# Attention heads: a third score buffer, one buffer for turned weights and value results, second scores in pieces

## The reference

```python
s = jnp.einsum('bqgrd,bkgd->bgrqk', qi, k).astype(jnp.float32) * scale
p = jax.nn.softmax(s, axis=-1).astype(v.dtype)
return jnp.einsum('bgrqk,bkgv->bqgrv', p, v)
```

## Time and profile before

| | us |
|---|---|
| median of 3 runs (2863.75 to 2866.16) | 2863.81 |
| the profiled execution | 2862.11 |
| its span, first to last instruction | 2860.3 |
| TensorE matmuls busy | 2600.9 (91%) |
| VectorE busy | 1240.2 (43%) |
| ScalarE busy | 1085.9 (38%) |
| GpSimd busy | 809.8 (28%) |
| DMA from HBM | 183.88 MB, mean 66 GB/s |

### The profile page before, as it was taken

How to read it: one execution, slowest core, us unless ns; L and a number is a source line. 1 busy time by engine, 2 the same in 40 slices (tenths; PEclk the granted TensorE clock), 3 DMA queues, 4 the chain that set the end, 5 groups by cost and what they waited for, 6 DMA issues and landing times. The chain is left out here.

```text
span 2860.3 us, 49221 instructions
## 1 busy us (share of the span) xinstructions
PE 2600.9 (91%) x19266; PEld 2041.7 (71%) x19266; DVE 1240.2 (43%) x1839; ACT 1085.9 (38%) x1682; POOL 809.8 (28%) x342
## 2 busy tenths in 40 slices
PE   8999979989898979888999999989978888998987
PEld 6887857868686857776778887767855566776665
DVE  3222024455655537344242220055846642584652
ACT  4443224343434323553233442233344422335441
POOL 3444433313232313112434444412210002232002
PEclk9999989999999989999999999999999999999998
DMA  4232322212121212111423233311110001121001
GB/s 135 90 95 92 105 66 86 91 52 83 59 83 59 83 39 74 52 38 59 134 82 95 88 95 98 100 37 53 55 41 1 1 9 51 52 74 59 1 1 66
DMA packets 52005, 188.49 MB, mean 66 GB/s; under 512 B 5760, under 2 KB 6016, under 8 KB 51712
## 3 DMA queue, kind: packets, MB, share of 16 engines
q1 hardware_dynamic: 50688, 181.74, 20.3%
q10 hardware_dynamic: 1152, 4.26, 0.4%
HBM read 183.88 MB, written 2.10 MB: 65 GB/s over the span
## 5 line engine op out<-in xcount | busy, mean ns | idle before, releaser
L2392 POOL TENSOR_TENSOR WLO<-RAW,WHI 128x1024 fp32r<-128x1024 f32 x334 | 804.7, 2409 | 2010.5 <-ACT WHI L299 2010.5
L299 ACT ACTIVATE WHI<-RAW 128x1024 fp32r<-128x1024 f32 x336 | 355.8, 1059 | 999.7 <-PE psum L313 708.8
L311 PE MATMUL psum<-HHI,WHI 128*128 128x512 f32 x872 | 353.8, 406 | 40.2 <-DVE HLO L397 15.0
L312 PE MATMUL psum<-HLO,WHI 128*128 128x512 f32 x872 | 347.0, 398 | 0.0
L313 PE MATMUL psum<-HHI,WLO 128*128 128x512 f32 x872 | 346.6, 397 | 0.0
L311 PE MATMUL psum<-H2HI,WHI 128*128 128x512 f32 (+1 forms) x536 | 197.3, 368 | 32.5 <-DVE H2LO L395 23.0
L311 PEld LDWEIGHTS psum<-HHI,WHI 128*128 128x128 f32 x872 | 165.8, 190 | 84.0 <-issue 43.9
L312 PEld LDWEIGHTS psum<-HLO,WHI 128*128 128x128 f32 x872 | 165.9, 190 | 41.7 <-issue 3.4
L313 PEld LDWEIGHTS psum<-HHI,WLO 128*128 128x128 f32 x872 | 165.7, 190 | 39.6
L312 PE MATMUL psum<-H2LO,WHI 128*128 128x512 f32 (+1 forms) x536 | 191.6, 357 | 0.0
L313 PE MATMUL psum<-H2HI,WLO 128*128 128x512 f32 (+1 forms) x536 | 191.2, 357 | 0.0
(11 more groups left out here) (394 smaller groups left out, 5196.6 us busy)
## 6 DMA issues: line engine op xcount, KB each, us to landing
RAW<-in_wstream SPq DMA_DIRECT2D x336, 512.0 KB, 3.5
X<-in_xT SPq DMA_DIRECT2D x8, 256.0 KB, 7.3
out_T<-OUT SPq DMA_DIRECT2D x4, 512.0 KB, 2.6
W3S<-in_lora ACTq DMA_DIRECT2D x5, 384.0 KB, 3.1
XC<-in_ctxT ACTq DMA_DIRECT2D x1, 1024.0 KB, 5.6
TRIG<-in_trig ACTq DMA_DIRECT2D x1, 960.0 KB, 7.6
FCC<-in_first SPq DMA_DIRECT2D x1, 576.0 KB, 9.0
LVL<-in_levels SPq DMA_DIRECT2D x1, 384.0 KB, 9.3
```

Of the source, the lines that this page charges most:

```text
L299: act.activation(WHI[:, q % 2, :], RAW[:, q % 2, :], ACT.Copy).then_inc(rounded, 1)
L311: pe.matmul(out, tile_of(WHI, slot, u), hi(kt), start=first and last[0], stop=False)
L312: pe.matmul(out, tile_of(WHI, slot, u), lo(kt), start=False, stop=False)
L2392: pool.tensor_tensor(WLO[:, s, :], RAW[:, s, :], WHI[:, s, :].bitcast(F32), ALU.subtract)\
```

## The change

There are three score buffers, `SCORES` = `two_banks` 0, 1 and 3, taken in turn by u % 3. There is one buffer for turned weights, `TURNED` = `two_banks[2]`, for even and odd units, and its columns 768 to 1023 hold the value results. So all turnings of an odd unit wait for the copy of the even one, and the turnings of an even unit for the copy of the odd unit before it. Its last two ("high") turnings, which share a bank with the value results, wait in addition for the result of the pair before.

TensorE's order for a pair with even unit u becomes: full scores of u + 2; values of the pair before; the four low turnings of u; the low scores (512 keys) of u + 3; the two high turnings of u; the high scores (256 keys) of u + 3; the six turnings of u + 1. The scores of units 0 and 1 stand ahead of the loop.

ScalarE does the exponents one unit ahead and then copies all 768 columns of a unit (256 for a context unit) in one instruction. VectorE copies no turned weights any more, and inverts the sums of a pair in one instruction of two columns. `heads_steps` is rewritten to these orders. The values wait for `ri` of the pair and for `pt` of the odd unit only.

```diff
@@ heads_tensor
+        SCORES, TURNED = (two_banks[0], two_banks[1], two_banks[3]), two_banks[2]
-            def scores(u):
+            def scores(u, ps):
...
-                    mm = pe.matmul(two_banks[a][:, at:at + w], lhs, rhs, start=True, stop=True)
-                mm.then_inc(*S.inc(f"sc{u}"))
+                    mm = pe.matmul(SCORES[u % 3][:, at:at + w], lhs, rhs, start=True, stop=True)
+                if ps and ps[-1][0]:
+                    mm.then_inc(*S.inc(f"sc{u}"))
             def values(j):
...
-                out = two_banks[3][:, TT:TT + 2 * P]
+                out = TURNED[:, TT:TT + 2 * P]
-                pe.wait_ge(*V.at(f"ri{2 * j + 1}"))
-                for u in (2 * j, 2 * j + 1):
-                    pe.wait_ge(*V.at(f"pt{u}"))
-                    pe.wait_ge(*A.at(f"pt{u}"))
+                pe.wait_ge(*V.at(f"ri{j}"))
+                pe.wait_ge(*A.at(f"pt{2 * j + 1}"))
...
-            scores(0)
-            for u, (kind, i, a, qb) in enumerate(us):
-                j = u // 2
-                if u + 1 < len(us):
-                    scores(u + 1)
-                if a == 0 and j:
-                    values(j - 1)
-                pe.wait_ge(*A.at(f"ex{u}"))
-                if a and j:
-                    pe.wait_ge(*V.at(f"y{j - 1}"))
-                pe.sem_inc(tensor_ready)
-                for b in keys_of(qb):
-                    mm = pe.transpose(two_banks[2 + a][:, b * P:(b + 1) * P], PX[:, a, b * P:(b + 1) * P], eye)
-                mm.then_inc(*S.inc(f"tr{u}"))
+            def turned(u, bs):
+                for b in bs:
+                    mm = pe.transpose(TURNED[:, b * P:(b + 1) * P], PX[:, us[u][2], b * P:(b + 1) * P], eye)
+                if KB - 1 in bs:
+                    mm.then_inc(*S.inc(f"tr{u}"))
+            LOW, HIGH = ((0, T),), ((T, TC),)
+            scores(0, LOW + HIGH)
+            scores(1, LOW + HIGH)
+            for u, (_, _, _, qb) in enumerate(us):
+                j, ahead = u // 2, u + 2 < len(us)
+                low, high = [b for b in keys_of(qb) if b < BLOCKS], [b for b in keys_of(qb) if b >= BLOCKS]
+                if u % 2 == 0:
+                    if ahead:
+                        if u:
+                            pe.wait_ge(*A.at(f"ex{u - 1}"))
+                        pe.sem_inc(tensor_ready)
+                        scores(u + 2, LOW + HIGH)
+                    if j:
+                        values(j - 1)
+                    pe.wait_ge(*A.at(f"ex{u}"))
+                    if u:
+                        pe.wait_ge(*A.at(f"pt{u - 1}"))
+                    pe.sem_inc(tensor_ready)
+                    if low:
+                        turned(u, low)
+                    if ahead:
+                        scores(u + 3, HIGH[:0] if us[u + 2][3] >= BLOCKS else LOW)
+                    if j:
+                        pe.wait_ge(*V.at(f"y{j - 1}"))
+                    pe.sem_inc(tensor_ready)
+                    turned(u, high)
+                    if ahead:
+                        scores(u + 3, HIGH)
+                else:
+                    pe.wait_ge(*A.at(f"ex{u}"))
+                    pe.wait_ge(*A.at(f"pt{u - 1}"))
+                    pe.sem_inc(tensor_ready)
+                    turned(u, low + high)
@@ heads_scalar
+            exponent(0)
             for u, (kind, i, a, qb) in enumerate(us):
...
+                if u + 1 < len(us):
+                    exponent(u + 1)
+                if a and j:
+                    rounded_part(j - 1)
                 act.wait_ge(*S.at(f"tr{u}"))
                 if j:
                     act.wait_ge(*S.at(f"pv{j - 1}"))
-                if qb < BLOCKS:
-                    act.activation(PTS[:, a, 0:T], two_banks[2 + a][:, 0:T], ACT.Copy).then_inc(*A.inc(f"pt{u}"))
-                else:
-                    act.sem_inc(A.inc(f"pt{u}")[0])
-                if a and j:
-                    rounded_part(j - 1)
+                act.activation(PTS[:, a, c0:], TURNED[:, c0:TT], ACT.Copy).then_inc(*A.inc(f"pt{u}"))
@@ heads_vector
             largest(0)
-            for u, (kind, i, a, qb) in enumerate(us):
+            largest(1)
+            for u in range(len(us)):
                 j = u // 2
-                if u:
-                    inverse(u - 1)
-                if u + 1 < len(us):
-                    largest(u + 1)
-                dve.wait_ge(*S.at(f"tr{u}"))
-                if j:
-                    dve.wait_ge(*S.at(f"pv{j - 1}"))
-                dve.tensor_copy(PTS[:, a, T:], two_banks[2 + a][:, T:TT]).then_inc(*V.inc(f"pt{u}"))
-                if j and not a:
+                if u % 2:
+                    inverse(j)
+                    if j:
+                        rest(j - 1)
+                if u + 2 < len(us):
+                    largest(u + 2)
+                if u % 2 == 0 and j:
                     result(j - 1)
-                if j and a:
-                    rest(j - 1)
```

More of the change, by code:

```diff
@@ L1696, in heads_steps @@
                 n = len(self.units())
-                pe, act, dve = ["sc0"], [], ["mx0", "nm0"]
+                pe, act, dve = ["sc0", "sc1"], ["ex0"], ["mx0", "nm0", "mx1", "nm1"]
                 for u in range(n):
-                    j = u // 2
-                    if u:
[L1701 to L1714, removed]
+                    j, ahead = u // 2, u + 2 < n
+                    if u % 2 == 0:
+                        pe += ([f"sc{u + 2}"] if ahead else []) + ([f"pv{j - 1}"] if j else []) + [f"tr{u}"]
+                        dve += ([f"mx{u + 2}", f"nm{u + 2}"] if ahead else []) + ([f"rg{j - 1}", f"y{j - 1}"] if j else [])
+                    else:
+                        pe += ([f"sc{u + 2}"] if ahead else []) + [f"tr{u}"]
+                        dve += [f"ri{j}"] + ([f"lo{j - 1}"] if j else []) + ([f"mx{u + 2}", f"nm{u + 2}"] if ahead else [])
+                    act += ([f"ex{u + 1}"] if u + 1 < n else []) + ([f"hi{j - 1}"] if u % 2 and j else []) + [f"pt{u}"]
                 j = n // 2 - 1
-                return pe + [f"pv{j}"], act + [f"hi{j}"], dve + [f"ri{n - 1}", f"rg{j}", f"y{j}", f"lo{j}"]
+                return pe + [f"pv{j}"], act + [f"hi{j}"], dve + [f"rg{j}", f"y{j}", f"lo{j}"]
         sa = Area(0)
@@ L2150, in heads_tensor @@
             st.enter(pe, "pe")
-            def scores(u):
+            def scores(u, ps):
                 kind, i, a, qb = us[u]
-                if u >= 2:
-                    pe.wait_ge(*A.at(f"ex{u - 2}"))
-                pe.sem_inc(tensor_ready)
                 hs = slice(a * HD, a * HD + HD)
                 qs = slice(qb * P, (qb + 1) * P)
-                for at, w in ((0, T), (T, TC)):
+                for at, w in ps:
                     if qb >= BLOCKS and not at:
@@ L2202, in heads_scalar, with exponent @@
             st.enter(act, "act")
+            def exponent(u):
+                kind, _, a, qb = us[u]
+                c0 = 0 if qb < BLOCKS else T
+                act.wait_ge(*V.at(f"nm{u}"))
+                if u >= 2:
+                    act.wait_ge(*S.at(f"tr{u - 2}"))
+                act.activation(PX[:, a, c0:], SCORES[u % 3][:, c0:TT], ACT.Exp, scale=scale_of(kind), bias=NM2[:, u % COLS:u % COLS + 1],
+                               accum_out=DEN2[:, u % COLS:u % COLS + 1]).then_inc(*A.inc(f"ex{u}"))
             def rounded_part(j):
@@ L2234, in largest, with inverse, part_of @@
                 dve.wait_ge(*S.at(f"sc{u}"))
-                dve.tensor_reduce(MX2[:, u % COLS:u % COLS + 1], two_banks[a][:, (0 if qb < BLOCKS else T):TT], AX, ALU.max).then_inc(*V.inc(f"mx{u}"))
+                dve.tensor_reduce(MX2[:, u % COLS:u % COLS + 1], SCORES[u % 3][:, (0 if qb < BLOCKS else T):TT], AX, ALU.max).then_inc(*V.inc(f"mx{u}"))
                 dve.wait_ge(*V.at(f"mx{u}"))
                 dve.tensor_scalar(NM2[:, u % COLS:u % COLS + 1], MX2[:, u % COLS:u % COLS + 1], -scale_of(kind), None, ALU.mult).then_inc(*V.inc(f"nm{u}"))
[L2238 to L2241, removed]
+            def inverse(j):
+                dve.wait_ge(*A.at(f"ex{2 * j + 1}"))
+                d = DEN2[:, 2 * j % COLS:2 * j % COLS + 2]
+                dve.reciprocal(d, d).then_inc(*V.inc(f"ri{j}"))
+            def part_of(t, j):
                 kind, i, _, qb = us[2 * j]
```

18 lines of the change are left out of this document (6 added, 12 removed).

## The result

The changed kernel takes **2863.75 us** (median of 20 runs, 2857.15 to 2870.12); the kernel before, run beside it, takes 2858.26 us (20 runs, 2852.22 to 2866.16). The ratio is 1.0019, 95% interval 1.0010 to 1.0027: 5.5 us slower, at the very edge (0.2%) of what I had said a measurement of this kernel can tell. The 2870.7 that I had forecast stands 12.4 us above the 2858.26 of before. The profiled execution of after took 2864.55 us, 2.4 more than that of before (2862.11).

The account below looks back on a forecast made before the run. TensorE, busy for 91% of the span, was taken as the bound. Layer 1's heads +4.9 us and layer 0's +2.0 made +6.9 on a profiled 2862.1, or 2869.0; 1.7 more for the median gave 2870.7 us, range 2860 to 2879.

Parts of the forecast that it names:

- the median of the runs is 1.7 higher: Last step of the total: 1.7 us added to the forecast profiled execution of 2869.0 us, giving 2870.7 us.
- "mla" pair: One full pair of "mla" units in the heads stages: 6.57 us against 6.44 before, +0.13.
- The stall behind the copy: Odd turning waits for ScalarE's whole even copy, starting at c + 1.42: stall of 0.72 us ("mla") and 0.43 ("gqa").
- "gqa" pair: One full pair of "gqa" units in the heads stages: 7.01 us against 6.47 before, +0.54.
- Edges: Start and end of each heads stage: −2.8 us in layer 1 (start −0.8, end −2.0), −1.6 in layer 0.
- Put at nothing: Stages outside the two heads stages: everything the change touches was taken to lie in the heads, so no term.
- No new wait of the values: Values in full pairs, due at 3.49 us with the odd copy ending at 3.18: 0.2 of slack, no new wait.
- VectorE's relief worth nothing: VectorE loses 120 copies (0.42 us each) and half its reciprocals; costed at nothing, since it isn't waited for.
- Stall covered: Rival at the odd turning: pieces hide the even copy, saving 0.72 or 0.43 us a steady step; 2851 us, chance 0.12.
- Shape changes overlap: Rival: low "gqa" piece costs 0.1 instead of 0.35 us and the clock holds at the edges; 2865 us, chance 0.11.
- Clock falls inside the loop: Rival: the 0.72 us gaps lower TensorE's clock, +5 us a pair, three such pairs giving 2886 us; chance 0.08.
- Nothing moves: Rival: copy and exponent trade places and the pair stays at 6.4 us; 2864 us, chance 0.05.

Follow-up runs that it names:

- The shared copy: Changed kernel with the copy of turned weights split, 512 columns by ScalarE and 256 by VectorE, context units staying with ScalarE; 2845.48 us (single run).
- the 128-row runs: Every "gqa" score taken from "mla" queries and keys, in the changed kernel (2846.89 us) and in the kernel before (2858.46 us), single runs.
- the swap: Changed kernel with the 256-key score piece ahead of the high even turnings and the 512-key piece behind them; 2850.86 us, ratio 0.9968 to before.
- the swap with the shared copy: Changed kernel with the two score pieces exchanged and the copy split between ScalarE and VectorE; 2843.55 us, ratio 0.9931 to before.
- the kernel with the longer stops: Changed kernel with no pieces, both score products of the odd unit behind the high even turnings; 2850.04 us, ratio 0.9973 to before.

## Why the prediction was right or wrong

**The sign was right, the time was not.** The time forecast, 2870.7, lies 12.4 us above the median of before as measured with it (2858.26); the change measured is +5.5 (+0.19% [0.10, 0.27]). The forecast is 7.0 above the 2863.75 measured, and two steps of it failed. The larger is the last step of the total, "the median of the runs is 1.7 higher" than before's profiled execution (2862.11): 20 runs put the median 3.9 *lower*, so this term was 5.6 too high. It rested on three runs. The other 1.4 is the sum of the change's terms (+6.9 against +5.5), and there the failed step is the "mla" pair: priced at +0.13 us, it costs nothing (6.43 against 6.44). The range, 2860 to 2879, holds the time near its lower end. As to the chances, the interval straddles my own bound of 0.2%, so the largest (slower by over 0.2%) and the second (within it) are both still possible.

**Term by term.**
- *The stall behind the copy* was right in kind and nearly in size: c + 1.42 forecast, 1.32 ("mla") and 1.38 ("gqa") measured. The copy took 0.81 as interpolated. It starts 0.41 behind c in "mla", where I had taken the 0.48 of context turnings, and its release takes 0.10 instead of 0.13. The shared copy shows that this wait sets the odd turning.
- *"mla" pair*: 6.57 forecast, 6.43 measured. 0.10 of it is that start and release, 0.04 the low scores (0.86, not 0.90). So the "mla" steps of layer 1 that keep to one kind cost nothing instead of +0.13 each. Of the change's own terms this is the one that was mis-sized: what it took for slower is no change.
- *"gqa" pair*: 7.01 forecast, 6.96 measured, and the cause (two more shape changes on the path) is shown by the 128-row runs. The 22 steps up to the last pair of layer 1 gave +5.6, where I had +7.7. Of these 2.1, the "mla" term is 0.9. The rest is the 0.05 of each full "gqa" step, the steps between the two kinds, which cost less than a full "gqa" one (6.62 and 6.77), and a slip in my sum: it has 23 steps in it (ten, twelve and the one into the last pair), one "gqa" step of +0.5 too many.
- *Edges*: layer 1's fill gave −0.9 (second pair's turning 11.74 after the start, forecast 11.9, before 12.68) and its drain −2.1 (forecast −2.0). For layer 0 I had −0.8 for the drain. Its last, context pair ran at the low clock in after (granted clock 0.50 in 2332 to 2338), so that the drain gained only 0.2. Its heads came out at +2.2 (forecast +2.0) only because the blocks cost a little less (34.42 and 34.70 from denominators to denominators, where I had 34.7 and 34.9): two misses that cancel, and so luck.
- *Put at nothing*: everything outside the heads. The 4.2 us behind layer 1's heads are most of why the two profiled spans lie closer together (2.5) than their heads (4.8). They come and go with the granted clock there, and not with the clock at which the heads end, as the rows above show; what sets it stays open.
- *No new wait of the values, VectorE's relief worth nothing*: both right in full pairs.

**The rivals.** *Stall covered* (2851): not so in the changed kernel, where 0.51 and 0.32 stay idle. But the price I gave it was real. With the pieces swapped and the copy shortened the stall is covered, the pairs come to 5.79 and 6.60 (my 6.57 and 7.01 less 0.72 and 0.43 are 5.85 and 6.58), and the time is 2844. *Shape changes overlap*: no, +0.53 a pair by the 128-row run. *Clock falls inside the loop*: not in the changed kernel's profile before its last context pair, and my reason (the gap of 0.72 in every pair, 0.62 as measured) was wrong, since the pairs with it kept a clock of 1.00. But it happened in three executions of two kernels (the swap, and the swap with the shared copy), behind context pairs, where TensorE has the least work. The Trainium skill, page "TensorE: Matmul & The Clock Gate", section "What's actually happening", says that the clock follows how busy the array has been lately. The place of the falls agrees with that. What doesn't follow from it in these rows is that TensorE then was busy without a break and stayed at 0.50 for some 17 us, and that the kernel with the longer stops kept 1.00. *Nothing moves*: true of "mla" alone, by the cancellation that this rival described.

**What I could have read and did not.** All numbers for swapping the pieces were in my sum: a wait of 0.72 at the odd turning beside a piece of 0.43, and a piece of 0.86 at a place where I had put no wait. I worked out what the order costs and never asked what the other order would.

## What to carry to other kernels

When work is cut in pieces to fill waits, list each wait with its length first and put the longest piece on the longest one; here the same instructions in the other order were worth 0.42 us a pair, the difference between slower and faster than before. A buffer given up makes TensorE wait for a copy, and what of that copy nothing covers is paid in full (0.21 less copy was 0.21 less pair), so shorten the copy (two engines) before giving a buffer up. Work whose array shape differs is dear in pieces unless both changes lie under a wait. Before a difference of 0.2% is read from whole times, measure the kernel before often: here the base moved by 5.6 us between 3 and 20 runs, as much as the change.

## What the runs showed that I had not expected

- The granted clock fell to 1.2 GHz for some 17 us in the middle of a stage, right where TensorE began a fully busy stretch, at a cost of 7.9 us, and in the same program it came or stayed away from one execution to the next (2838.82 us without, 2847.11 with, for swap and shared copy).
- A second stop of 0.42 us in the context pairs stood ahead of each fall, in three of the four executions that had it. A kernel with a stop of 1.05 us there kept its clock, so the stop alone isn't the cause.
- The output projection behind layer 1's heads, and all after it, took from 66.6 to 70.9 us with none of their instructions changed, and started at a granted clock of 1.00, 0.66 or 0.50. Which of these it was did not follow from the clock at which the heads ended.
